# Inverting 64x64 blocks through their 32x32 diagonal blocks, with the full Gram products between the levels

## The chip, the core and the metric

The kernel runs on one core of one Trainium2 chip. The metric is the device time of one execution in microseconds (us). The core's engines run their own queues side by side and meet at semaphores: TensorE (PE; weight loads are shown apart as PEld), VectorE (DVE), ScalarE (ACT), GpSimd (POOL) and SyncE (SP), which issues most DMAs.

## What is computed

Two stacks of two layers on 256 tokens of width 1024. The first block (attention, spatial gating, a mixture of 64 experts) isn't touched. Each layer of the second block is `x + 0.5 swiglu(x)`, a mixer, and again `x + 0.5 swiglu(x)`. The mixer runs two branches on the projections of the normed x: differential attention over 4 head pairs, and an RWKV-7 recurrence in both directions over 8 heads of 64 channels:

```python
def step(state, inp):
    r_t, w_t, k_t, v_t, kk_t, a_t = inp
    sa = jnp.einsum('bhvk,bhk->bhv', state, -kk_t)
    state = (state * w_t[:, :, None, :]
             + sa[..., None] * (kk_t * a_t)[:, :, None, :]
             + v_t[..., None] * k_t[:, :, None, :])
    y_t = jnp.einsum('bhvk,bhk->bhv', state, r_t)
    return state, y_t
```

The result y gets a group norm, `ln_x`, the bonus `(r . k . r_k) v` and a gate; then `merged = sigmoid(gate_a) (o_a @ w_branch[0]) + sigmoid(gate_b) (o_b @ w_branch[1])`, and x + merged @ w_out. All is float32.

## The kernel before

The recurrence is cut into 4 chunks of CH = 64 tokens. Within a chunk, the effect of the sa terms on one another is a unit triangular 64x64 matrix for each head, chunk and direction, 64 of them a layer, whose inverse is wanted. They lie as two blocks in the 128 partitions and 8 columns of blocks (`u`), in four groups i = 2d + q: direction d, head half q. float32 matmuls stand in the trace as two pairs of weight load and matmul each.

The stages of one layer's mixer, all in `second_block`. Each engine has its own function (`tensor`, `scalar`, `vector`, `gpsimd`, `sync`), in which the order is written by hand, and `plan` deals the 8 PSUM banks out in the same order (`banks.take`); `claim` makes TensorE wait until a bank is freed, `read` makes another engine wait until it is filled, `evacuated` waits for the free.

- *Attention beside gates.* `score`, `turn_comb`, `values` of the 8 score tiles and 4 heads, with the gate projections in halves (`half_gates(i)`, L2122: 8 matmuls of 128x256) between them. VectorE makes softmax terms (`biased`, `combine`) and the scaled operands A, B, K, R (`keys`, `scaled`). TensorE waits for `kk_scaled` (L3040) before the products `kkb` (L2325), then come `score(2)`, the transposes of V and `half_gates(0)`. After `values(3)` come the token transposes (L2365) and the bonus sums (L2403).
- *Gram products* (`gram`, L2383 and L2379): UR and KR, 64x128 each, and L, 64x64, for each of the 64 blocks, masked out of PSUM by VectorE (`masked`: L3148, L3151) into UM, KM and X. GpSimd builds the start of the inverse and of its transpose from them (L2070 to L2072). The transposes of the attention output (`obT`, L2089) stand between the third and the fourth group and wait for VectorE's norm of it (`ob_ready`, L3169).
- *Levels*: five doublings on whole 64x64 blocks. In each, VectorE masks the level's part of U into Z (L3158), TensorE makes W = Z' X (`own_blocks`, L2393), ScalarE copies it to W1, TensorE makes dX and dXT, and VectorE adds them (L3188, L3192). One call of `own_blocks` is 16 matmuls of 64x64, 32 pairs, over two of the four 64x64 tiles of the array.
- *Q1, Atok, SA0, XAT* (L2443, L2450, L2393, L2467), all copied by ScalarE.
- *Scan* over 4 chunks (L2530 to L2549, L2480), with half_gates 10 to 13 one behind each chunk; then half_gates 14 and 15, the gate product (L2569), VectorE's group norm chain (L3243 to L3266), the transposes of the result (L2089), and `branch` (L2583), whose 8 output tiles each take 4 matmuls with either branch weight.

## Time and profile before

| | |
|---|---|
| median of 3 runs | 3445.56 us (3436.99 to 3446.21) |
| the profiled execution | 3436.36 us, its span 3434.5 us |
| TensorE busy | 3151.6 us, 92% |
| VectorE, ScalarE, GpSimd busy | 1494.9, 802.7, 636.4 us |
| mean granted TensorE clock | 0.946 of 2.4 GHz |
| the first layer's stage from the first Gram product to the scan | 2248 to 2344 us |
| the same in the second layer | 3022.5 to 3118 us |

Durations in a timeline row are those of a merged group: the number behind x is how many instructions it holds, and in brackets stands how long the engine was idle before it and who released it. The granted clock is given as a share of 2.4 GHz; it has two levels, 1.0 and 0.5.

### The profile page before, as it was taken

What the parts mean: (1) busy time and instruction counts of PE and PEld (TensorE: products, weight loads), DVE (VectorE), ACT (ScalarE), POOL (GpSimd) and SP (SyncE); (2) the same over time, 40 slices, a digit from 0 to 9 for tenths busy, and PEclk for the clock granted to TensorE, in tenths of its full rate; (3) what the DMA queues carried; (4) which work ended last, traced back from release to release, by engine and by line L of the source; (5) the groups of instructions that cost most, each with busy time, mean ns of one, the idle gap of its engine ahead of it and who ended that gap; (6) DMA issues with size and microseconds to landing.
All of it is one profiled execution on the core that took longest, in us unless ns stands there. A gap on an engine that the chain in (4) does not pass through costs nothing. (4 is left out here: it accounts for less than half of the span.)

```text
span 3434.5 us, 51714 instructions
## 1 busy us (share of the span) xinstructions
PE 3151.6 (92%) x22119; PEld 2147.9 (63%) x22119; DVE 1494.9 (44%) x2451; ACT 802.7 (23%) x1128; POOL 636.4 (19%) x580
## 2 busy tenths in 40 slices
PE   7988999999788889999994999988999999988999
PEld 3765334433256553334442998787798898787798
DVE  2334333323353243233325556673454655773454
ACT  1211111111013011111111335422233434522232
POOL 3511233333155022333332000020000000020000
PEclk9978999999888889999997999899999999999999
DMA  8635999999966369999997543202454553202452
GB/s 296 239 114 216 407 376 395 385 383 377 371 224 232 142 254 402 380 379 385 380 383 287 198 170 117 74 27 93 154 184 159 192 174 139 74 27 88 156 188 86
DMA packets 305358, 799.19 MB, mean 233 GB/s; under 512 B 57038, under 2 KB 155876, under 8 KB 251244
## 3 DMA queue, kind: packets, MB, share of 16 engines
q1 hardware_dynamic: 245804, 727.16, 56.3%
q0 software_dynamic: 58784, 66.64, 5.9%
q8 instruction: 177, 2.90, 0.3%
q10 hardware_dynamic: 544, 2.10, 0.2%
q14 instruction: 49, 0.40, 0.0%
HBM read 988.60 MB, written 53.48 MB: 303 GB/s over the span
## 5 line engine op out<-in xcount | busy, mean ns | idle before, releaser
L808 PE MATMUL f_bank<-f_ringA,f_arena 128*64 128x512 f32 x3072 | 688.0, 601 | 14.8 <-DMA f_ringA<-in_w_up,f_chosen 10.4
L808 PEld LDWEIGHTS f_bank<-f_ringA,f_arena 128*64 128x64 f32 x3072 | 218.3, 138 | 404.4 <-issue 403.3
L2133 PE MATMUL s_bank<-s_hT_parts,s_highA_parts 128*128 128x256 f32 x1344 | 380.7, 283 | 0.0
L2133 PE MATMUL s_bank<-s_hT_high_parts,s_ringA_parts 128*128 128x256 f32 x1344 | 380.6, 283 | 0.0
L2133 PE MATMUL s_bank<-s_hT_high_parts,s_highA_parts 128*128 128x256 f32 x1344 | 380.6, 283 | 0.0
L829 PE MATMUL f_bank<-f_ringB,f_arena 128*64 128x512 f32 x1536 | 346.3, 592 | 2.1 <-DVE f_arena L1595 2.1
L1580 DVE TENSOR_TENSOR f_arena<-f_arena,f_bank 128x256 f32<-128x256 f32 x96 | 58.7, 612 | 594.0 <-ACT f_arena L1190 594.0
L1111 ACT ACTIVATE f_arena<-f_bank 128x512 f32<-128x512 f32 (+1 forms) x266 | 144.8, 583 | 605.6 <-PE f_bank L789 323.3
L2133 PEld LDWEIGHTS s_bank<-s_hT_high_parts,s_highA_parts 128*128 128x128 f32 x1344 | 258.2, 192 | 1.4
L2133 PEld LDWEIGHTS s_bank<-s_hT_parts,s_highA_parts 128*128 128x128 f32 x1344 | 258.1, 192 | 1.4
L2133 PEld LDWEIGHTS s_bank<-s_hT_high_parts,s_ringA_parts 128*128 128x128 f32 x1344 | 258.1, 192 | 0.0
L829 PEld LDWEIGHTS f_bank<-f_ringB,f_arena 128*64 128x64 f32 x1536 | 112.3, 137 | 218.6 <-issue 216.0
L2930 DVE TENSOR_TENSOR s_ringA_parts<-s_ringA,s_highA_parts 128x4096 fp32r<-128x4096 f32 x44 | 194.7, 4424 | 61.2 <-ACT s_highA_parts L2624 60.9
L1589 DVE TENSOR_TENSOR f_arena<-f_bank,f_gate_b 128x512 f32<-128x512 f32 x192 | 132.9, 692 | 173.8 <-PE f_bank L829 156.9
L1190 ACT ACTIVATE f_arena<-f_bank 128x256 f32<-128x256 f32 x96 | 36.9, 385 | 657.8 <-PE f_bank L808 657.8
L2942 DVE TENSOR_TENSOR s_ringB_parts<-s_arena,s_highB_parts 128x2048 fp32r<-128x2048 f32 x44 | 100.8, 2292 | 193.4 <-ACT s_highB_parts L2634 193.1
L2624 ACT ACTIVATE s_highA_parts<-s_ringA 128x4096 fp32r<-128x4096 f32 x44 | 159.1, 3615 | 91.5 <-DMA s_ringA<-in_ffn_in 77.1
L2634 ACT ACTIVATE s_highB_parts<-s_arena 128x2048 fp32r<-128x2048 f32 x44 | 84.2, 1914 | 389.9 <-PE s_bank L2203 382.8
L2612 ACT ACTIVATE s_arena<-s_bank 128x512 f32<-128x512 f32 (+2 forms) x178 | 99.3, 577 | 259.3 <-PE s_bank L2393 87.2
L769 PE MATMUL f_bank<-f_hT,f_ringA 128*128 128x256 f32 x640 | 157.3, 409 | 2.7 <-ACT f_arena L1111 2.7
L682 POOL DMA_INDIRECT y_rows<-f_arena,f_rows_of x96 | 100.9, 1051 | 290.4 <-PE f_bank L789 231.8
L2070 POOL TENSOR_TENSOR s_arena<-s_arena,s_masks 128x512 f32<-128x512 f32 x8 | 11.1, 1383 | 747.2 <-DVEq L3153 747.2
(416 smaller groups left out, 5145.7 us busy)
## 6 DMA issues: line engine op xcount, KB each, us to landing
f_ringA<-in_w_gate SPq DMA_DIRECT2D x128, 1024.0 KB
f_ringA<-in_w_up SPq DMA_DIRECT2D x128, 1024.0 KB
f_ringB<-in_w_down SPq DMA_DIRECT2D x128, 1024.0 KB
s_ringA<-in_ffn_in SPq DMA_DIRECT2D x88, 1024.0 KB, 7.7
f_ringA<-in_w_ada SPq DMA_DIRECT2D x46, 1024.0 KB, 13.4
s_arena<-in_ffn_out SPq DMA_DIRECT2D x44, 1024.0 KB, 6.5
s_ringA<-in_w_in SPq DMA_DIRECT2D x40, 1024.0 KB, 6.2
f_ringA<-in_w_in SPq DMA_DIRECT2D x28, 1024.0 KB, 14.0
```

The lines of the kernel that those rows point to most:

```text
L682: pool.indirect_dma_start(out=a["y_rows"], out_offset=bass.IndirectOffsetOnAxis(ap=row_out[:, b:b + 1], axis=0), in_=y_tok[:, b % 3, :, :] ...
L769: last = mm(ps[:, t * S:(t + 1) * S], w[:, k, t * P:(t + 1) * P], hT[:, k, :], start=(k == 0), stop=(k == DT - 1))
L808: last = mm(ps[j * CAP:(j + 1) * CAP, :].rearrange("p (h c) -> p h c", h=2), picked[:, b % 2, k, j * CAP:(j + 1) * CAP], gu[j][:, :, k, :] ...
L829: last = mm(ps[j * CAP:(j + 1) * CAP, :], hidT[:, k, j * CAP:(j + 1) * CAP], wd[j][:, k, n * 512:(n + 1) * 512], start=(k == 0), stop=(k = ...
L1111: banks.free(f(dst, view(banks.read(act, key)), func), key)
L1589: banks.free(tt(y_tok[:, (b - 1) % 3, n, :], ps[:, :], gate_b[:, n * 512:(n + 1) * 512], ALU.mult), key)
L2133: last = mm(ps[:, t * S:(t + 1) * S], parts_of(wx[:, k, cs_]), parts_of(hx[:, k, :]), start=(k == 0 and x == 0), stop=(k == DT - 1 and x = ...
L2612: banks.free(f(dst, view_(banks.read(act, key)), func, **kw), key)
L2624: f(parts_of(highA[:, s % 2, :]), slotA(n), ACT.Copy).then_inc(highA_ready, 1)
L2634: f(parts_of(highB[:, s % 2, :]), ringB[:, s % B_SLOTS, :], ACT.Copy).then_inc(highB_ready, 1)
L2930: tt(parts_of(w), w, parts_of.value(highA[:, s % 2, :]), ALU.subtract).then_inc(lowA_ready, 1)
L2942: tt(parts_of(w), w, parts_of.value(highB[:, s % 2, :]), ALU.subtract).then_inc(lowB_ready, 1)
```

## The change

On VectorE, ScalarE and TensorE the inversion now works on the two 32x32 diagonal blocks of each 64x64 block (SUB = 32), through four levels, and a last step makes the off-diagonal 32x32 block. In detail:

- Small Gram products (`small_gram`) give L and U of the diagonal 32x32 blocks alone, side by side in one bank per (q, hh). ScalarE copies U to Uc, VectorE masks the start X and its transpose XX out of the same bank and adds the unit. GpSimd's twelve operations a layer are gone, and the L products of 64x64.
- A level handles both directions together: for each q one W of 64 matmuls (`quarters`: 32x32 blocks over the four diagonal tiles), one copy by ScalarE, and for each group one bank D with both updates, 64 matmuls, added by VectorE in one operation. VectorE's level mask covers both directions.
- The 16 full Gram products UR and KR (one bank each, `gram(name, d, q, hh)`) stand four to a level between W and D; VectorE masks them there. They were ahead of the levels.
- The last step: `last_level_left` (W5), `inverse_whole` (a selecting matmul of 256 columns puts the diagonal blocks into PSUM), `last_level_right` (adds the off-diagonal part), copied by ScalarE and VectorE to XT. The obT transposes follow.
- VectorE takes half of the copies of Q1, Atok, SA0 and XAT.
- Order on TensorE: kkb behind half_gates(0); bonus and the first token transposes ahead of half_gates(8); the small Gram products ahead of turn_comb(3), which moves combine(3) on VectorE behind the first start masks; half_gates 12 and 13 from the scan to its end.
- `branch` goes by weight: four tiles with the first, the same four with the second, then the other four; each weight is waited for where it is first used.
- VectorE: two of the operations behind the scan (bonus times V, plus the bias) are done ahead of it into yadd, and the mean's scaling is folded into the subtraction. ScalarE takes the square root for the group norm ahead of the last two gate copies, and runs the early gates' sigmoids in levels 2 and 3.

```diff
-        LEVELS = 5
+        LEVELS = 4
         scan_order = [list(range(NCH)), list(range(NCH))[::-1]]
         GATES_EARLY = 5
+        fillers = [(name, d, q, hh) for name in ("UR", "KR") for d in range(2) for q in range(2) for hh in range(2)]
...
                 pool.wait_ge(tables_landed, 4 * 16)
-                step = Chain(pool, pool_steps)
-                add = nc.gpsimd.tensor_tensor
-                unit = spread(masks[:, 12, :], 1, 8)
-                for d in range(2):
-                    for q in range(2):
-                        pool.wait_ge(u_ready, 2 * d + q + 1)
-                        step(add(XT[d][:, q], UM[d][:, q, :, 0, :], spread(masks[:, 6, :], 1, 8), ALU.mult))
-                        step(add(X[d][:, q], X[d][:, q], unit, ALU.add))
-                        add(XT[d][:, q], XT[d][:, q], unit, ALU.add).then_inc(start_ready, 1)
                 leave(pool, l)
...
-                half_gates(6)
-                turn_comb(2)
-                half_gates(7)
-                values(2)
-                half_gates(8)
-                turn_comb(3)
-                half_gates(9)
-                values(3)
...
+                def small_gram(q):
+
+                    ps = [banks.claim(pe, ("LU", q, hh)) for hh in range(2)]
+                    for d in range(2):
+                        for x in range(2):
+                            for a in range(2):
+                                for c in range(NCH):
+                                    for r in range(2):
+                                        s = slice(c * CH + r * SUB, c * CH + (r + 1) * SUB)
+                                        o = c % 2 * CH + r * SUB
+                                        n = 8 * d + 4 * x + 2 * a + c // 2
+                                        for hh in range(2):
+                                            h = slice(hh * HD, hh * HD + HD)
+                                            sides = AR[d][h, 2 * q + a, 0, s], Bt[d][h, 2 * q + a, s]
+                                            last = mm(ps[hh][o:o + SUB, n * SUB:(n + 1) * SUB], sides[x], sides[1 - x],
+                                                      start=True, stop=True)
+                                            if n == 15 and r == 1 and c == NCH - 1:
+                                                banks.fill(last, ("LU", q, hh))
+
+                def quarters(ps, at, left, right):
+
+                    for u in range(8):
+                        for o in range(0, P, SUB):
+                            last = mm(ps[o:o + SUB, (at + u) * SUB:(at + u + 1) * SUB], left[o:o + SUB, u],
+                                      right[o:o + SUB, u], start=True, stop=True)
+                    return last
 
...
+                tokens_first(0)
+                half_gates(8)
+                pe.wait_ge(ABKR_ready, 2)
+                for q in range(2):
+                    small_gram(q)
+                turn_comb(3)
+                half_gates(9)
+                values(3)
                 tokens_first(1)
-                gram(1, 0)
+
+                filler = iter(fillers)
+                for lv in range(LEVELS):
+                    for q in range(2):
+                        pe.wait_ge(z_ready, 2 * lv + q + 1)
+                        if lv:
+                            for i in (q, 2 + q):
+                                banks.evacuated(pe, ("D", i, lv - 1))
+                        else:
+                            pe.wait_ge(start_ready, 2 * q + 2)
+                        ps = banks.claim(pe, ("W", q, lv))
+                        for d in range(2):
+                            last = quarters(ps, 8 * d, Z[:, q, d], XX[d][:, q, 0])
+                        banks.fill(last, ("W", q, lv))
+                        gram(*next(filler))
+                    for q in range(2):
+                        banks.evacuated(pe, ("W", q, lv))
+                        for d in range(2):
+                            i = 2 * d + q
+                            ps = banks.claim(pe, ("D", i, lv))
+                            quarters(ps, 0, XX[d][:, q, 1], W1[:, q, d])
+                            banks.fill(quarters(ps, 8, W1[:, q, d], XX[d][:, q, 1]), ("D", i, lv))
+                        gram(*next(filler))
+
...
+                                src, to = o + d * SUB, o + (1 - d) * SUB
+                                other = slice((1 - d) * SUB, (2 - d) * SUB)
+                                last = mm(ps[to:to + SUB, u * SUB:(u + 1) * SUB], UM[d][src:src + SUB, q, u, 0, other],
+                                          XX[d][src:src + SUB, q, 0, u], start=True, stop=True)
+                    banks.fill(last, ("W5", q))
...
+                        ps = banks.claim(pe, ("XF", q, r))
+                        for d in range(2):
+                            for o in (0, CH):
+                                src = slice(o + r * SUB, o + (r + 1) * SUB)
+                                mm(ps[o:o + CH, d * S:(d + 1) * S], ident[src, o:o + CH],
+                                   XX[d][src, q, 1].rearrange("p u t -> p (u t)"),
+                                   start=True, stop=False, skip_group_check=True)
...
+                                r = 1 - d
+                                ps = banks.t[banks.uses[("XF", q, r)][0]]
+                                src, to, at = o + r * SUB, o + d * SUB, d * S + u * SUB
+                                last = mm(ps[to:to + SUB, at:at + SUB], W5[src:src + SUB, q, u],
+                                          XX[d][src:src + SUB, q, 1, u], start=False, stop=True, skip_group_check=True)
+                                if u == 7 and o == CH:
+                                    banks.fill(last, ("XF", q, r))
+
+                last_level_left(0)
+                inverse_whole(0)
+                last_level_left(1)
...
-                    half_gates(2 * GATES_EARLY + n)
+                    if n < 2:
+                        half_gates(2 * GATES_EARLY + n)
                 pe.wait_ge(sa_ready, 2 * (NCH - 1))
                 for d in range(2):
                     last = from_steps(d, NCH - 1)
                     banks.fill(last, ("YA", scan_order[d][NCH - 1] // 2))
-                half_gates(14)
-                half_gates(15)
+                for i in range(12, 16):
+                    half_gates(i)
                 for m in range(MT):
                     ps = banks.claim(pe, ("gate", m))
...
-                for t in range(DT):
-                    ps = banks.claim(pe, ("branch", t))
+                for first in (0, 4):
                     for half, (n, src) in enumerate(((a_wa, oaT), (a_wb, obT))):
+                        landed(n)
                         w = slotA(n).rearrange("p (k c) -> p k c", k=4)
-                        for k in range(4):
-                            last = mm(ps[:, half * S:(half + 1) * S], w[:, k, t * P:(t + 1) * P], src[:, k, :],
-                                      start=(k == 0), stop=(k == 3))
-                    banks.fill(last, ("branch", t))
+                        for t in range(first, first + 4):
+                            ps = banks.t[banks.uses[("branch", t)][0]] if half else banks.claim(pe, ("branch", t))
+                            for k in range(4):
+                                last = mm(ps[:, half * S:(half + 1) * S], w[:, k, t * P:(t + 1) * P], src[:, k, :],
+                                          start=(k == 0), stop=(k == 3))
+                            if half:
+                                banks.fill(last, ("branch", t))
...
+                def start_whole(i):
+
+                    xx = XX[i // 2][:, i % 2].rearrange("p x u t -> p (x u) t")
+                    for hh in range(2):
+                        banks.evacuated(dve, ("LU", i % 2, hh))
+                    tt(xx, xx, spread(small_masks[:, 4, :], 1, 16), ALU.add).then_inc(start_ready, 1)
+                        combine(3)
+                    for i in (q, 2 + q):
+                        start_whole(i)
                 for m in range(MT):
                     ps = banks.read(dve, ("o", m))
                     banks.free(v.tensor_copy(ob[:, m, :], ps[:, :]), ("o", m))
                     banks.evacuated(dve, ("o", m))
...
+                def level_mask(q, lv):
+
+                    of_level = small_masks[:, 5 + 2 * lv:7 + 2 * lv, :].unsqueeze(2).broadcast_to([P, 2, 8, SUB])
+                    tt(Z[:, q], Uc[:, q], of_level, ALU.mult).then_inc(z_ready, 1)
+
+                banks.evacuated(dve, "bonus")
+                filler = iter(fillers)
+                for q in range(2):
+                    level_mask(q, 0)
+                for lv in range(LEVELS):
+                    for _ in range(2):
+                        masked(*next(filler))
+                    for q in range(2):
+                        if lv < LEVELS - 1:
+                            banks.read(dve, ("W", q, lv))
...
-                step(ts(small[:, 120:136], small[:, 120:136], 1.0 / HD, None, ALU.mult))
-                step(tt(t1, yh, spread(small[:, 120:136], 2, HD), ALU.subtract))
+                step(stt(t1, spread(small[:, 120:136], 2, HD), -1.0 / HD, yh, ALU.mult, ALU.add))
...
                 step(tt(ym, ym, spread(lnx[:, 0, :], 1, MT), ALU.mult))
-                step(tt(ym, ym, spread(lnx[:, 1, :], 1, MT), ALU.add))
-                step(tt(t2, Vtok.rearrange("p m (h d) -> p (m h) d", d=HD), spread(small[:, 240:256], 2, HD),
-                        ALU.mult))
-                step(tt(ytmp, ytmp, ytmp2, ALU.add))
+                step(tt(ytmp, ytmp, yadd, ALU.add))
```

## Rows read from the trace of the kernel before

**Rows 1.** The page's busy times of the whole span.
```profile
PE 3151.6 (92%) x22119; PEld 2147.9 (63%) x22119; DVE 1494.9 (44%) x2451; ACT 802.7 (23%) x1128; POOL 636.4 (19%) x580
```

**Rows 2.** Busy time by stage, second block's mixer; columns in the first line.
```profile
core 0: us, PE busy (x) PEld busy (x) DVE busy (x) ACT busy (x) POOL busy (x), PEclk, DMA share, GB/s
...
2248.00:2272.00 24.00, 17.48 (x411) 16.08 (x411) 18.28 (x27) 5.04 (x9) 12.73 (x9) 0.79 0.01 3
...
2285.00:2297.00 12.00, 12.00 (x419) 12.00 (x416) 9.00 (x13) 2.91 (x5) 0.00 (x0) 1.00 0.02 4
...
2272.50:2330.20 57.70, 54.51 (x1792) 54.13 (x1794) 40.98 (x56) 15.94 (x26) 4.45 (x3) 0.97 0.02 4
...
2330.20:2343.90 13.70, 12.62 (x407) 11.48 (x402) 0.74 (x2) 9.56 (x24) 0.00 (x0) 1.00 0.02 5
...
2380.60:2400.80 20.20, 10.87 (x46) 8.36 (x45) 14.28 (x16) 4.38 (x7) 0.00 (x0) 0.84 0.60 218
...
3046.50:3104.30 57.80, 54.18 (x1804) 53.83 (x1797) 41.50 (x58) 15.93 (x26) 5.16 (x4) 0.97 0.02 4
```

**Rows 3.** Timeline of the Gram stage: start, duration, engine, line, operands, idle before.
```profile
2265.38 1.97 PE L2089 MATMUL s_bank<-ident,s_arena 128*128 128x128 f32 x8 [5.52 <-DVE s_arena L3169]
```

**Rows 4.** Timeline, weight loads: 128 columns, 64 at full and at half clock.
```profile
2244.45 3.09 PEld L2403 LDWEIGHTS s_bank<-s_rksel,s_arena 128*128 128x128 f32 x27
...
2257.39 1.76 PEld L2383 LDWEIGHTS s_bank<-s_arena 64*64 64x64 f32 x64 [0.24 <-issue]
...
2259.08 0.64 PEld L2379 LDWEIGHTS s_bank<-s_arena 64*64 64x64 f32 x32
...
2267.57 3.32 PEld L2383 LDWEIGHTS s_bank<-s_arena 64*64 64x64 f32 x64 [0.62 <-issue]
```

**Rows 5.** DMA queues, 2285 to 2330: the instruction queue's packets, MB, share.
```profile
q8 instruction: 11, 0.18, 1.7%
```

**Rows 6.** Timeline before the Gram stage, TensorE and VectorE.
```profile
2187.88 3.78 PE L2325 MATMUL s_bank<-s_arena,s_headselT 8*128 8x256 f32 x8 [4.15 <-DVE s_arena L3040]
...
2209.49 0.66 PE L2302 MATMUL s_bank<-ident,s_arena 128*128 128x128 f32 x4 [0.54 <-DVE s_arena L3082]
...
2233.68 1.05 PE L2312 MATMUL s_bank<-s_arena 128*128 128x128 f32 x8
...
2235.64 0.88 DVE L3082 SCALAR_TENSOR_TENSOR s_arena<-s_arena,s_small 128x256 f32<-128x256 f32 x2
```

**Rows 7.** Busy time by stage at the low clock (columns as in rows 2).
```profile
2247.70:2251.10 3.40, 3.40 (x57) 3.38 (x60) 0.53 (x1) 1.68 (x3) 0.00 (x0) 0.50 0.02 5
...
2268.00:2271.00 3.00, 3.00 (x64) 3.00 (x60) 1.08 (x3) 0.00 (x0) 2.40 (x2) 0.50 0.00 0
...
2394.50:2404.70 10.20, 5.89 (x17) 4.76 (x18) 3.26 (x4) 1.19 (x2) 0.00 (x0) 0.50 1.04 388
```

**Rows 8.** Timeline, changes of tile shape behind the levels.
```profile
2331.25 0.66 PE L2450 MATMUL s_bank<-ident,s_arena 128*128 128x128 f32 x4
...
2331.83 1.01 PEld L2443 LDWEIGHTS s_bank<-s_arena 64*64 64x64 f32 x32 [0.17 <-issue]
```

**Rows 9.** Groups by line, 1500 to 3434: VectorE on 128x512.
```profile
L3158 DVE TENSOR_TENSOR s_arena<-s_arena,s_masks 128x512 f32<-128x512 f32 x40 | 36.7, 936 | 7.3 <-PE s_bank L2393 6.7
...
L3192 DVE TENSOR_TENSOR s_arena<-s_bank,s_arena 128x512 f32<-128x512 f32 x40 | 27.7, 692 | 15.2 <-PE s_bank L2393 15.2
```

**Rows 10.** Timeline after the scan.
```profile
2380.59 7.17 PE L2122 MATMUL s_bank<-s_hT,s_ringA 128*128 128x256 f32 x32
...
2381.87 1.39 DVE L3243 TENSOR_TENSOR s_arena<-s_bank,s_arena 64x512 f32<-64x512 f32 x2 [7.49 <-ACT s_arena L2612]
...
2394.02 1.22 DVE L3261 TENSOR_TENSOR s_arena<-s_arena,s_small 128x1024 f32<-128x1024 f32 x1
...
2397.93 1.97 PE L2089 MATMUL s_bank<-ident,s_arena 128*128 128x128 f32 x8 [8.45 <-DVEq L3269]
...
2400.78 24.40 PE L2583 MATMUL s_bank<-s_arena,s_ringA 128*128 128x256 f32 x103 [0.89 <-ACT s_arena L2612]
```

More of the change, by code:

```diff
@@ L1667, in second_block @@
         masks = sb("masks", [P, 13, CH])
+        SUB = CH // 2
         dist = sb("dist", [P, MT, S])
@@ L2334, in tensor @@
                 half_gates(0)
+                pe.wait_ge(kk_scaled, 1)
+                for g in range(2):
+                    ps = banks.claim(pe, ("kkb", g))
+                    for t in range(2):
+                        last = mm(ps[:, t * S:(t + 1) * S], headselT[:, 2 * g + t, :], kk_norm, start=True, stop=True)
+                    banks.fill(last, ("kkb", g))
                 score(3)
@@ new lines, in scalar @@
+                take("bonus", bonus, lambda ps: ps[:, 0:16].rearrange("p (m h) -> p m h", m=MT))
+                tokens_first(0)
+                for q in range(2):
+                    for hh in range(2):
+                        ps = banks.read(act, ("LU", q, hh))[:, :].rearrange("p (d x n t) -> p d x n t", d=2, x=2, n=4)
+                        f(Uc[:, q, :, 4 * hh:4 * hh + 4, :], ps[:, :, 1], ACT.Copy).then_inc(u_ready, 1)
+                combined(3)
+                take_gates(4, ACT.Copy)
@@ new lines, in scalar @@
+                take(("Q1", 0), Q1[0], lambda ps: ps[:, :].rearrange("p (u c) -> p u c", u=8))
+                for q in range(2):
+                    ps = banks.read(act, ("XF", q, 0))
+                    for d in range(2):
+                        f(XT[d][:, q, :, 0:SUB], ps[:, d * S:(d + 1) * S].rearrange("p (u t) -> p u t", u=8), ACT.Copy
+                          ).then_inc(inv_ready[0], 1)
+                    act.wait_ge(inv_ready[0], 2 * q + 2)
+                    banks.free(act.nop(), ("XF", q, 0))
```

412 lines of the change are left out of this document (220 added, 192 removed).

## The prediction

> **What bounds the kernel now.** I read the busy shares first: TensorE is busy 92% of the span [rows 1], so the question is which work leaves its queue, and where it stands idle. The busy table by stage [rows 2] cuts the second block's mixer of the first layer (the second repeats it 774 us later; its level stage is the last row there). The level stage, 2272.5 to 2330.2, takes 57.7 us at 94% busy, with VectorE at 41 and ScalarE at 16: TensorE bounds it by instruction count, 1792 pairs of weight load and matmul, 29 ns each (12 us for some 415 of them). The Gram stage before it, 2248 to 2272, is bound by waits: TensorE is busy 17.5 of 24 us at a mean clock of 0.79, and its longest stop, 5.5 us, is for the vector chain that ends in L3169 [rows 3]. A third idle place, after the scan, is taken up in step 4.
>
> **The pace of a 32x32 pair** decides the change, and no row shows one. Its ends come from the loads' start spacing [rows 4]. Weight loads of 128 columns on the whole array come every 112 ns (3.09 us for 27). Loads of 64 columns come every 29 ns with two array tiles in use [rows 2], so 58 ns for each tile, and every 16 ns with four (0.64 us for 32, less the last one's own 0.13): 64 per tile. Per tile the time is a straight line in the columns: 58 at 64, 112 at 128, so 31 at 32. With the four diagonal tiles of a 32x32 block that is 7.8 ns per pair: the lower end. The upper end is 16, about the closest that pairs ever stand over a group of 32. Code loading lies between: eleven 16 KB blocks in 45 us took 1.7% of 16 engines, 1.1 us each [rows 5]; the 3584 instructions of the level stage are 254 a block at that rate. Loaded one behind the other, that is 8.7 ns per pair. I take 10, nearest to this row with a little room.
> The Trainium skill speaks against the change here: "TensorEngine Tiling (Array Packing)", section Instruction Overhead, says that each matmul carries about 60 cycles, so that 1 and 60 columns cost the same. That is 25 ns at 2.4 GHz; the 16 ns of the four-tile group does not agree with it as a limit on the queue.
>
> **The change part by part, one layer.** Times are those of the first layer.
> 1. *Before the levels.* Now the levels begin at 2272.5. VectorE is busy almost without a gap to 2236.5 (its third combine, L3082) and TensorE follows it: the first comb transpose starts on its release at 2209.49, and the third head's values start at 2233.68 [rows 6]. Moving score, V transposes and the first gate half ahead of the kk wait covers 4.15 us of idleness, but the same time is idle again before that comb transpose: nothing gained, -1 to +2 for a colder start. From the end of the values at 2234.6: bonus 4.0, first token transposes 1.9 plus 1.5 because the clock falls behind the bonus (it fell to 0.50 at 2247.7, right after it [rows 7]), half a gate 3.6, and 256 pairs of small Gram products at 10 ns, 2.5: 2248.1. These have two halves of rows and four of columns in use, 4 to 16 ns a pair: 1.0 to 4.1. VectorE's third combine now stands behind the first two start masks: copy on ScalarE 0.75, four masks of 0.41, combine 2.1: 2252.6. Behind that TensorE has transposes 0.6, half a gate 3.6, values 1.05: 2257.8; VectorE's two copies of o (1.4) and one level mask (0.7), with 0.3 of signalling, put the first level at 2260.2. That is 12.3 earlier, and neither GpSimd's start chain nor the obT transposes are before it.
> 2. *Levels.* Five levels become four. Each has 256 pairs in W and 512 in the two updates, 7.7 us at 10 ns, against 384 before: twice the instructions. Four full Gram products ride in each as fillers: 16 pairs of 128 columns over two tiles. Four tiles took 27 ns a pair at full clock (1.76 us for 64 [rows 4]), so two take 53: 0.85 us each, 3.4 in all. Each filler changes the tile shape twice. A change from 64x64 to 128x128 costs 0.16 us between loads [rows 8]; eight cost 1.4 with rounding up, 0 if these two shapes need none. A level is 12.5 us, four are 50.0 against 57.7. The Trainium skill ("TensorEngine Tiling (Array Packing)", Key Properties) states that changing the tiling mode drains the array; the 0.16 us agrees.
> Cover: VectorE has ten operations of 128x512 a level, 0.69 each as L3192 [rows 9], 7.2 us; L3158 took 0.94 in the mean only beside GpSimd, which is now idle. Group norm work adds 2.7 us behind level 0 and 2.9 in level 2. Total 34.5 of 50, so no stall until a pair falls below 7. ScalarE's two copies have a filler and the other W behind them. Range of the four levels: 43 (7.8 ns; 38 if the shape changes are free) to 68 (16).
> 3. *From the levels to the scan*, 13.7 us now. The last level, which joins the two 32-wide halves, is 256 pairs (2.6) and 32 selecting pairs of 256 columns over two tiles, 107 ns each (3.4). Moved here from the Gram stage are the obT transposes, 0.9. The rest is as now: four Q1 and four SA0 of 0.93 each, 3.7 and 3.7, XAT 4 times 0.5, transposes 1.7, eleven shape changes 1.8, final wait 1.3. Sum 21.1: 7.4 later. VectorE takes half of the copies, 3.0 us a pair of heads against 4.6 on TensorE. The two new yadd operations (1.22 each, as L3261 [rows 10]) stand before the first state, 0.9 us late, behind which TensorE has from_keys and half a gate: nothing.
> 4. *After the scan.* Two of the gate halves leave it: VectorE's answers have landed behind the remaining from_steps, so the scan ends 7.2 earlier (four halves then follow; two take 7.17 [rows 10]). They run beside the norm chain, where TensorE waits 8.45 now. From the last YA product, branch starts at 20.2 now [rows 2]. After: gates 14.4, gate product 1.9, VectorE's last gate multiply 0.9, transposes 1.0, copies 1.0: 19.3. The chain itself loses 2.7 us (three operations) and is no longer last. The branch's first 4 us run at half clock now, since the clock is 0.50 from 2394.5 to 2404.7 [rows 7]; without the idleness 2.0 are saved. Splitting branch by weight hides the second weight load: it is issued when the last gate ends, +14.4, and has until about +26.7. Sum: -10.1.
> **Sum.** -12.3 - 7.7 + 7.4 - 10.1 = -22.7 a layer, -45 in two. Against the profiled execution, 3436.4 us, that is 3391. This execution lies 9 below the median of the runs, 3445.6, so I put the median after at **3400**.
>
> **Rivals.**
> *A, the array's own line (7.8 ns or a little more).* 3328 pairs a layer hang on the pace, plus 256: 3.6 us for each ns. 2.2 ns less are 16 us in two layers: 3384. For: pairs in a group start together, waiting for the tile only. Against: no longer stretch shows it.
> *B, the sequencer or code loading holds about 14 to 16 ns.* 3.6 x 2 x 4 to 6 = +29 to +43: 3429 to 3443. Break-even is at 16.3 ns. For: it is the closest spacing seen. Against: that spacing is just what four 64-column tiles allow.
> *C, slower: the clock falls in the levels.* The clock fell behind the bonus though its loads kept the queue full (8 columns each), and in the gappy start of the levels; the 32-column pairs use a sixteenth of the array each. At half clock a pair is 16 ns and a filler 1.7 (64 pairs took 3.32 us for 1.76 [rows 4], the clock at 0.50 there [rows 7]): 20.5 us a level, +32 a layer: 3464. It eats the whole gain when about 70% of the level time is at the low level. Against: the 64x64 pairs, a quarter of the array each, hold 1.00 for 50 us, and the fillers stand between.
> *D, slower by far: the queue delivers no faster than now.* 29 ns is the only pace that the trace holds over hundreds of pairs; if it is the queue's and not the tiles', each 32x32 pair costs it: 19 x 3.6 x 2 = +137: 3537. For: the groups at 16 ns are only 32 pairs long and could be drawn from a filled queue. Against: they stand at it right behind long stretches at 29. With the 25 ns of the Trainium skill ("TensorEngine Tiling (Array Packing)", Instruction Overhead) the same mechanism would give 3508.
> *E, steps 1 to 3 don't do what they say:* waits that the sum doesn't have eat them and only step 4 stays, 10 us a layer: 3425, beside B.
>
> **How the numbers follow.** Forecast (9 to 12 ns) 0.42, 3386 to 3417; A 0.20; B with E 0.24; C in part or whole 0.10; D 0.04. Of C about a half is a partial fall that leaves the time within or below the old one. A with free shape changes and a good early stage reaches 3372; B ends at 3443. Range 3372 to 3443. A measurement here tells 0.3%, 10 us, from no change. Faster by more than that: forecast, A and most of B, 0.77; within: the end of B, part of C, 0.12; slower: C, D, 0.11.
>
> **What would show it.** The level stage: four levels, each with 768 pairs, length 50 us; the spacing of the 32x32 loads, 10 ns; granted clock 1.00 in it. The levels' start 12 us earlier relative to the comb transposes; TensorE idle some 4 us before the last comb transpose. The stage from the last level to the scan at 21 us. After the scan, no idle time over 1.5 us on TensorE until branch, and full clock in it. GpSimd with no tensor operation, VectorE's level masks at 0.69. The prediction is wrong if the pairs stand at over 13 ns, if VectorE or ScalarE ends the waits in the levels, or if the clock is 0.50 in them.

## The result, and the profile after

| | us | |
|---|---|---|
| before | 3441.56 | median of 4 runs, 3436.99 to 3446.21 |
| after | 3506.24 | median of 4 runs, 3498.87 to 3507.56 |
| ratio | 1.018 | 95% interval 1.016 to 1.021 |
| profiled execution after | 3507.32 | span 3505.5, mean clock 0.923 (before: 0.946) |

The change costs 65 us. The forecast was a gain of some 45, and the time is outside its range. The page of after, busy times and the instruction queue, to be read against [rows 1]:

```profile
PE 3193.1 (91%) x26023; PEld 2170.6 (62%) x26023; DVE 1456.2 (42%) x2425; ACT 789.6 (23%) x1104; POOL 599.0 (17%) x556
...
q8 instruction: 207, 3.39, 0.4%
```

TensorE has 3904 more pairs of load and matmul than before. In the table of the first layer's stages (columns as in [rows 2]) the rows are: the small Gram products, the four levels, the way to the scan, the scan, and the stretch from the last YA product to branch:

```profile
2247.40:2260.00 12.60, 5.87 (x513) 5.42 (x512) 4.57 (x13) 0.66 (x2) 0.00 (x0) 0.66 0.02 4
2270.00:2366.90 96.90, 76.26 (x3329) 67.29 (x3328) 30.34 (x44) 10.55 (x17) 0.00 (x0) 0.54 0.02 4
2366.90:2388.80 21.90, 20.40 (x697) 17.28 (x697) 7.92 (x18) 8.49 (x21) 0.00 (x0) 0.91 0.02 5
2388.80:2418.50 29.70, 28.53 (x673) 26.27 (x673) 10.85 (x24) 0.60 (x1) 0.00 (x0) 1.00 0.20 73
2418.50:2437.20 18.70, 16.84 (x77) 13.67 (x77) 11.75 (x13) 6.15 (x9) 0.00 (x0) 1.00 0.18 60
```

Against [rows 2]: the levels begin 2.5 us earlier (2270.0 for 2272.5), last 96.9 us in place of 57.7, the way to the scan takes 21.9 for 13.7, and from the scan's start on 10.4 us are won (scan 29.7 for 36.7, stretch to branch 18.7 for 20.2, branch itself 27.9 for 29.8). That is -2.5 + 39.2 + 8.2 - 10.4 = +34.5 us a layer, 69 in two; the two profiled executions differ by 71.0. So **the whole loss, and more, is in the level stage**, where VectorE is busy 30 and ScalarE 11 of 97 us.

What TensorE waits for there stands in the costliest groups (busy us, mean ns of one, then idle time before it and its releaser), both layers together:

```profile
L2391 PE MATMUL s_bank<-s_arena 32*32 32x32 f32 x6144 | 94.6, 233 | 36.2 <-issue 36.0
L2364 PE MATMUL s_bank<-s_arena 64*64 64x128 f32 x512 | 61.1, 403 | 5.0 <-issue 4.9
L2382 PE MATMUL s_bank<-s_arena 64*32 64x32 f32 x1024 | 11.8, 229 | 12.8 <-issue 12.8
```

"Issue" is a stop for nothing that the profile shows: no engine, no data. In the first layer's level stage these stops sum to 20.6 us. The timeline tells their rhythm. First the small Gram products (L2382), then the beginning of the levels (start, duration, line, count, idle before):

```profile
2247.43 1.74 PE L2382 MATMUL s_bank<-s_arena 64*32 64x32 f32 x182
2251.44 1.61 PE L2382 MATMUL s_bank<-s_arena 64*32 64x32 f32 x128 [2.27 <-issue]
2255.32 1.55 PE L2382 MATMUL s_bank<-s_arena 64*32 64x32 f32 x128 [2.26 <-issue]
2259.06 1.04 PE L2382 MATMUL s_bank<-s_arena 64*32 64x32 f32 x74 [2.20 <-issue]
...
2270.01 1.29 PE L2391 MATMUL s_bank<-s_arena 32*32 32x32 f32 x128
2271.22 0.66 PE L2364 MATMUL s_bank<-s_arena 64*64 64x128 f32 x8
...
2280.84 1.74 PE L2391 MATMUL s_bank<-s_arena 32*32 32x32 f32 x128 [0.53 <-issue]
2284.59 0.39 PE L2391 MATMUL s_bank<-s_arena 32*32 32x32 f32 x25 [2.00 <-issue]
...
2288.32 1.93 PE L2391 MATMUL s_bank<-s_arena 32*32 32x32 f32 x128 [0.69 <-issue]
2292.34 0.79 PE L2391 MATMUL s_bank<-s_arena 32*32 32x32 f32 x41 [2.09 <-issue]
```

Two things are to be seen. At the full clock 128 of the 32x32 pairs are through in 1.21 us (2270.01 to 2271.22), 9.5 ns each: the pace that was forecast at 10. And TensorE stops for 2 us again and again, each time 128 pairs, 256 instructions, after the last stop. 256 instructions are one 16 KB packet of the instruction queue; in the level stage (2270.0 to 2366.9) this queue has 26 of them (packets, MB, share):

```profile
q8 instruction: 26, 0.43, 1.9%
```

Put beside each other, the starts of TensorE's instructions counted in 256s, and the starts of the packets in that queue (both from the trace, us; the stop here runs from the start of one instruction to the start of the next, so it is some 0.2 longer than the idle time in brackets above):

```
after, levels
block taken up at   stop before it   own work of the block before   next packet starts   and takes
2251.44             2.47             1.08                           +1.14                1.29
2255.32             2.50             1.37                           +1.16                1.11
2259.06             2.43             1.31                           +1.07                1.38
2284.59             2.19             1.55                           +1.41                1.07
2292.34             2.33             1.69                           +1.18                0.94
2299.52             0.00             3.57                           +1.41                0.88
2307.09             2.05             1.69                           +1.12                1.36
```

A packet starts some 1.15 us after TensorE has taken up a block, moves in 0.9 to 1.4, and TensorE goes on 2.6 us after the packet's start. So the next block can be taken up some 3.75 us after this one (3.5 to 4.3 over the stage, its first block apart, which took 2.9). If this block has 3.6 us of work there is no stop (the sixth line, at the half clock); if it has 1.5, TensorE stands for the rest. The level stage has 4 x 1664 = 6656 instructions, 26 blocks: 26 x 3.75 = 97.5 us, and it took 96.9. At the half clock, though, many blocks of this stage have just 3.6 us of work of their own, so this sum alone doesn't tell blocks from the clock; the experiments have to.

The rule of the Trainium skill that bears on it ("Runtime: NRT & Kernel Launch", section Instruction fetch mechanics) says that a queue of the sequencer's own loads the next 16 KB block while the present one is executed; the table agrees. It also says that this is hidden, because instructions issue more slowly than the blocks come; that does not hold here: 256 instructions of these pairs are executed in 1.3 us and their successors come in 3.75.

### The profile page after: what moved, and what is told of

The parts are those of the page before. It is cut to its first block and busy times, and to the rows that moved or that the text cites. A ratio compares the mean times of both kernels' runs of the same rounds, so it can differ in the third digit from the quotient of the medians.

```text
span 3505.5 us, 59420 instructions
## 1 busy us (share of the span) xinstructions
PE 3193.1 (91%) x26023; PEld 2170.6 (62%) x26023; DVE 1456.2 (42%) x2425; ACT 789.6 (23%) x1104; POOL 599.0 (17%) x556
## 5 line engine op out<-in xcount | busy, mean ns | idle before, releaser
L2701 ACT ACTIVATE s_arena<-s_bank 128x512 f32<-128x512 f32 (+2 forms) x142 | 78.9, 575 | 324.2 <-PE s_bank L2391 139.1
L769 PEld LDWEIGHTS f_bank<-f_hT,f_ringA 128*128 128x128 f32 x640 | 131.4, 207 | 27.2 <-ACT f_arena L1111 4.0
```

The source lines that it names most:

```text
L769: last = mm(ps[:, t * S:(t + 1) * S], w[:, k, t * P:(t + 1) * P], hT[:, k, :], start=(k == 0), stop=(k == DT - 1))
L2701: banks.free(f(dst, view_(banks.read(act, key)), func, **kw), key)
```

## The experiments

Theories: **T1**, TensorE waits for blocks of instructions; **T2**, the clock, 0.54 in the levels, makes them long; **T3**, each 32x32 product has its price in the array. The kernel before alone took 3425 to 3448 us over all its runs, so a difference of some 10 us between two single runs says nothing; the stage lengths are surer.

**Same instructions, twice the array work (`wide`).**

```diff
                     for u in range(8):
+                        v = u // 2 * 2
                         for o in range(0, P, SUB):
-                            last = mm(ps[o:o + SUB, (at + u) * SUB:(at + u + 1) * SUB], left[o:o + SUB, u],
-                                      right[o:o + SUB, u], start=True, stop=True)
+                            last = mm(ps[o:o + SUB, (at + v) * SUB:(at + v + 2) * SUB], left[o:o + SUB, u],
+                                      right[o:o + SUB, v:v + 2].rearrange("p u t -> p (u t)"), start=True, stop=True)
```

> The kernel after, with each 32x32 product of the levels made 64 columns wide (it reads and writes two neighbouring products' columns), so the values of the levels are wrong, and the number of instructions is the same: 4 levels of 832 loads and 832 matmuls, with the array's work in them doubled. Theory T1 (TensorE waits for its instructions, which come in blocks of 256, one every 3.75 us, whatever it computes): the four levels stay at 4 x 1664 / 256 x 3.75 = 97 us a layer, the kernel within 10 us of 3506, even if the granted clock in the levels rises from 0.50. Theory T2 (the half clock makes the levels long: the 32x32 pair takes 14.6 ns there and 9.4 ns at the full clock, and the idle gaps keep the clock low): more columns keep the clock up or, at the half clock, take 53 ns for a pair of two streams' worth, so the levels move by over 10 us either way. Theory T3 (a price of each 32x32 product in the array): doubled columns lengthen the levels, by up to 3072 x 13 ns = 40 us a layer at the full clock, kernel over 3550.

Measured: 3495.45 us, beside 3434.11 for before on that chip. The level stage of this kernel:

```profile
2261.00:2356.70 95.70, 70.10 (x3331) 61.60 (x3331) 30.34 (x44) 10.51 (x17) 0.00 (x0) 0.97 0.02 5
```

95.7 us with the array doing double and the clock at 0.97, against 96.9 at 0.54: T3 falls. The kernel is 11 us below after, a little more than T1 allowed, but 9 of these are there before the levels begin (2261.0 for 2270.0), ahead of any changed product. T2 has a way out that its wording missed: twice the columns at twice the clock would also take as long as before. What closes it is the idle time. TensorE is busy 70.1 of the 95.7 us, and the 25.6 us between are "issue" stops at every 256th instruction, as in after. Both layers' small products in the costliest groups:

```profile
L2392 PE MATMUL s_bank<-s_arena 32*32 32x64 f32 x6144 | 109.1, 224 | 45.0 <-issue 45.0
```

From 2261.0 to 2312.7 the clock is 1.00 throughout, and 15.1 us of such stops lie in these 51.7 us, so T2 falls too.

**Half the instructions, the same columns (`half`).** As `wide`, with `for u in range(0, 8, 2)`.

> The kernel after, with every second 32x32 product of the levels left out and the others 64 columns wide, so the values are wrong; the levels stream the same number of columns with 448 loads and 448 matmuls in place of 832 each. T1 (instruction blocks): 4 x 896 / 256 x 3.75 = 52.5 us of levels a layer in place of 97, the kernel at about 3506 - 2 x 44.5 = 3417. T2 (half clock, set by the columns streamed): the levels stay near 97 us if the clock stays at 0.50, the kernel near 3506.

Measured: 3419.1 us, 2 over T1's number. The level stage:

```profile
2270.10:2321.60 51.50, 43.26 (x1792) 36.92 (x1790) 29.79 (x44) 10.59 (x17) 0.00 (x0) 1.00 0.02 5
```

51.5 us where 14 blocks were to take 52.5, and the same columns streamed. By length alone the three stages would also fit columns streamed, divided by the clock (131 thousand columns at 0.54, 229 at 0.97, 131 at 1.00: 96.9, 95.7 and 51.5 us); the idle time, 25.6 us in `wide` and 8.2 here, at nearly the full clock, is what such a rule has no place for. Together with it, these lengths say that the number of instructions sets the time.

**Large useless products between the levels (`ballast`).** In the function of the full Gram products:

```diff
+                    for _ in range(2):
+                        mm(ps[:, :], ident[:, :], AR[d][:, 2 * q, :, :].rearrange("p r s -> p (r s)"), start=True, stop=True)
                     for a in range(2):
```

> The kernel after, with two useless 128x128 by 512-column products ahead of each of the 16 Gram products between the levels (32 a layer, two passes each, written to the bank that the Gram product then overwrites): 64 x 0.213 us = 13.7 us more work of TensorE a layer at the full clock, twice that at the half clock, in only 128 instructions, half a block. T1 (instruction blocks come at their own pace while TensorE computes): the levels stay at 97 us, at most 2 us more for the half block, and the work lies in the waits; the kernel within 5 us of 3506. T2 and T3 (TensorE is busy with the array's work in the levels): 14 us more a layer, the kernel at 3534; under T2 less where the clock comes back.

Measured: 3554.99 us, 49 over after's own median, where I expected no more than 5. Both halves of the expectation were off. A pass of 512 columns takes 0.5 us at the full clock and 0.85 at half, not 0.213, so the added work was some 45 us a layer:

```profile
L2361 PE MATMUL s_bank<-s_arena,ident 128*128 128x512 f32 x128 | 89.8, 839 | 0.9 <-issue 0.9
L2393 PE MATMUL s_bank<-s_arena 32*32 32x32 f32 x6144 | 70.0, 201 | 46.4 <-issue 46.4
```

Of these 45 us, 24 lengthened the level stage:

```profile
2272.70:2393.80 121.10, 96.71 (x3394) 61.84 (x3392) 30.32 (x44) 10.60 (x17) 0.00 (x0) 0.82 0.02 4
```

The rest did not go into the waits: TensorE is idle 24.4 us of this stage, where it was 20.6 in after. It was given back by the clock, 0.82 for 0.54, at which the stage's own products took some 25 us less. So the stops are all still there, 46 us in two layers. The timeline shows why:

```profile
2299.56 0.66 PE L2393 MATMUL s_bank<-s_arena 32*32 32x32 f32 x53 [2.48 <-issue]
2300.15 3.48 PE L2361 MATMUL s_bank<-s_arena,ident 128*128 128x512 f32 x4
...
2324.06 1.31 PE L2393 MATMUL s_bank<-s_arena 32*32 32x32 f32 x128 [1.12 <-issue]
2327.81 0.33 PE L2393 MATMUL s_bank<-s_arena 32*32 32x32 f32 x8 [2.43 <-issue]
2328.07 3.53 PE L2361 MATMUL s_bank<-s_arena,ident 128*128 128x512 f32 x4
...
2335.38 0.44 PE L2393 MATMUL s_bank<-s_arena 32*32 32x32 f32 x29 [1.80 <-issue]
```

The block taken up at 2327.8 has 5.6 us of own work and is followed by a stop all the same. The packets show why, if one counts how many of a block's instructions stand ahead of its first large product:

```
ballast, levels of both layers (us)
block taken up at   instructions ahead of the large product   next packet   next block
2369.08             10                                         +4.63         +7.04
2327.80             16                                         +4.99         +7.57
2279.40             24                                         +4.79         +7.37
3130.48             39                                         +5.30         +7.98
2379.59             51                                         +1.26         +7.21
2335.38             58                                         +1.05         +3.97
2290.24             65                                         +1.29         +5.55
2299.56            106                                         +1.07         +5.63
2295.79             none in this block                         +0.87         +3.77
```

The next block is asked for when TensorE's queue is some 40 to 50 instructions into the present one (late at 39, in time at 51). A large product ahead of that point holds the request back by its whole time and hides nothing; behind that point it hides up to 2 us. And nothing is loaded further ahead than one block: the block at 2346.68 took 5.6 us without a stop behind it, and yet the short one after it, at 2352.30, had to wait 2.1 us for its successor. So T1 was refined: each block costs the longer of about 3.75 us and its own work, one by one, and what a block has too much does nothing for the next.

**The same kind of work in small portions (`even`).** In the function of the 32x32 products:

```diff
+                    for _ in range(2):
+                        mm(ps[:, at * SUB:(at + 8) * SUB], ident[:, :], AR[0][:, 0, 0, :], start=True, stop=True)
                     for u in range(8):
```

> The kernel after, with useless work of TensorE again, now in small portions: two 128x128 by 256-column products ahead of every 32 of the 32x32 products, written to the columns that these then overwrite. By the run with 512 columns a pass of 512 took about 0.5 us at the full clock and 0.85 at half, so a pass of 256 about 0.25 to 0.43; 48 portions of 4 passes a layer are 48 to 82 us more work a layer, with 384 more instructions, 1.5 blocks. Theory T1 as the 512-column run leaves it (each block of 256 instructions is asked for when TensorE takes up the one before, is there 3.75 us later, and nothing is loaded further ahead, so a block costs the longer of 3.75 us and its own work): a block's work is 1.2 to 1.5 us and 2.0 to 2.3 portions, 3.3 to 3.8 us at the full clock, so nearly all of the added work lies in the waits: the levels 97 + 5.6 (1.5 blocks) = 100 to 112 us, the kernel 3515 to 3536. If blocks were loaded any number ahead, the levels are also near 103 us, and then the 16 large portions of the other run should have cost nothing, which they did not. If TensorE's own work fills the levels: 97 + 48 to 82 us, the kernel over 3600.

Measured: 3521.2 us. The level stage, and the groups of the useless and of the small products:

```profile
2273.10:2377.10 104.00, 101.80 (x3577) 77.91 (x3577) 31.03 (x45) 9.74 (x15) 0.00 (x0) 1.00 0.02 4
...
L2390 PE MATMUL s_bank<-s_arena,ident 128*128 128x256 f32 x384 | 108.3, 405 | 0.1
L2393 PE MATMUL s_bank<-s_arena 32*32 32x32 f32 x6144 | 74.4, 194 | 1.9 <-issue 1.5
```

54 us of useless work a layer lengthen the stage by 7 (1.5 blocks more would be 5.6), and nearly all stops in it are gone: TensorE is idle 2.2 us for 20.6. Some 18 of the 54 us thus lie in the former stops, and some 28 were offset by the clock, 1.00 for 0.54, at which the stage's own products take less. The expectation had put nearly all into the stops, so its number came out (3515 to 3536) in part for another reason, and by its time alone this run doesn't tell blocks from the clock; that rests on `wide`. It tells one more thing: the stage is now 98% busy at clock 1.00, so without the useless work the levels' own work is 104 - 54, some 50 us. That is the number of the prediction's step 2; it was TensorE's own work at the full clock, and that was not what bound.

**Do the old levels wait for instructions too?** Their pace, 29 ns a pair [rows 2], is also 3.7 us for 256 instructions. First half of the columns (`narrow`): `own_blocks` got a width, 32 in levels 1 to 4.

> The kernel before, with the 64x64 products of levels 1 to 4 streaming 32 columns in place of 64, so the values are wrong; the number of instructions is the same (896 products a layer, 3584 instructions). T1 (instruction blocks bind the old levels too): the level stage stays at 57.7 us, the kernel at 3441 plus or minus 5. If the array's time for a 64x64 product was the bound of the old levels, the 704 narrowed ones, two passes each, save up to 1408 x 13 ns = 18 us a layer, the kernel at about 3405.

Measured: 3438.34 us, T1's number, but the trace speaks against T1's reason:

```profile
2281.72 50.49 PE L2393 MATMUL s_bank<-s_arena 64*64 64x64 f32 x1696 [1.69 <-issue]
```

1696 pairs in one piece with no stop in it, 29.8 ns each, though most of them stream half the columns: neither streamed columns nor visible waits. Its weight loads kept their 64 columns; no run varies these alone. Then useless work ahead of each 16 products of the old kernel (`before_even`):

```diff
                 def own_blocks(ps, left, right):
+                    mm(ps[:, 0:S], ident[:, :], AR[0][:, 0, 0, :], start=True, stop=True)
```

> The kernel before, with one useless 128x128 by 256-column product (two passes, 0.265 us each at the full clock by the run even) ahead of each of the 60 calls that make 16 of the 64x64 products: 32 us more work a layer, 64 in all, with 240 more instructions a layer. If the array holds the old levels at 29 ns a product and instructions are only just in time (128 products take 3.7 us, the block's own 3.75), the work adds in full: the kernel at 3500. If the old levels too wait for their instructions, in a form that shows no pauses, the work lies in these waits: the kernel below 3450.

Measured: 3524.59 us beside 3424.82: the work adds in full, 100 us where its array time alone was put at 64. The timeline (the useless passes are L2391):

```profile
2360.29 1.15 PE L2394 MATMUL s_bank<-s_arena 64*64 64x64 f32 x32
2361.37 0.70 PE L2391 MATMUL s_bank<-s_arena,ident 128*128 128x256 f32 x2
2362.00 1.15 PE L2394 MATMUL s_bank<-s_arena 64*64 64x64 f32 x32
2363.08 0.70 PE L2391 MATMUL s_bank<-s_arena,ident 128*128 128x256 f32 x2
```

A call has 32 pairs, 0.94 us at 29.2 ns, and comes every 1.71 here: 0.77 more, 92 us for 120 calls, no part of it hidden. The instruction packets now come 5.3 to 7.4 us apart, so no block is waited for here, and 32 products still take 1.15 us. So it is the products themselves that hold the old levels at 29 ns, and their instructions come only just in time: 3.7 us of work for a block that takes 3.75. (In the second layer of `obt_late`, below, the old levels show two stops labelled "issue", 0.18 and 0.23 us, 126 pairs apart.) What in the products the 29 ns are, if not the columns streamed, stays open; the 64-column weight load is the candidate that no run tested.

**The edits behind the scan alone (`scan_end`).** Its diff is that of the change, limited to the gates' order and banks, branch by weight, and the bonus term and the shift made during the scan.

> The kernel before with the change's edits behind the scan alone: the halves of the gates 12 to 15 behind the scan, the gates' last group in another bank, ScalarE's roots ahead of the last two gate groups, VectorE's bonus term and shift made during the scan, one VectorE step in place of two, the branch matrices taken by weight. The levels stay as they were. The prediction's step 4 had 10.1 us a layer for these, 20 us in all: the kernel at 3421. If the gain of step 4 hung on the rest of the change, or the edits only move a wait: within 5 us of 3441.

Measured: 3413.38 us against 3434.59, ratio 0.994, interval 0.992 to 0.995: 21 us faster, 20 expected. Its end of the scan:

```profile
2376.20 14.08 PE L2123 MATMUL s_bank<-s_hT,s_ringA 128*128 128x256 f32 x64
2390.12 1.88 PE L2571 MATMUL s_bank<-s_g,s_arena 128*128 128x512 f32 x4
2392.82 1.09 PE L2090 MATMUL s_bank<-ident,s_arena 128*128 128x128 f32 x8 [0.83 <-DVEq L3273]
```

The four gate halves (first row) lie beside VectorE's norm chain, and the 8.45 us idle of [rows 10] are 0.83.

**A start for the old levels.** `obt_late` is `scan_end` with the obT transposes moved behind the levels, and VectorE's norm of them behind its last Gram masks, to take away the 5.5 us of [rows 3].

```diff
                 gram(1, 0)
-                pe.wait_ge(ob_ready, 1)
-                to_features(("obT",), ob, 2)
                 gram(1, 1)
...
+                pe.wait_ge(ob_ready, 1)
+                to_features(("obT",), ob, 2)
                 for m in range(MT):
```

> scan_end, and the 16 transposes of the second half's output moved from between the Gram products to behind the levels, with VectorE's five norm steps ahead of them moved behind its last Gram mask. TensorE waited 5.5 us there a layer and the transposes took some 2 us: if the Gram products bound the start of the levels, 7 us a layer less than scan_end, 3407; if VectorE's masks and GpSimd's starts bind it anyway, 0 to 3 us a layer, 3415 to 3421.

Measured: 3409.91 us, ratio 0.994, interval 0.992 to 0.995: not to be told from `scan_end`. The Gram products end early, and TensorE then stands before the fourth product, until GpSimd's last start value is there (its last row ends at 2269.4):

```profile
2267.08 2.33 POOL L2073 TENSOR_TENSOR s_arena<-s_arena,s_masks 128x512 f32<-128x512 f32 x1
...
2269.51 15.70 PE L2394 MATMUL s_bank<-s_arena 64*64 64x64 f32 x458 [4.10 <-issue]
```

Here "issue" does hide an engine: the row above names it. `start_split` is `obt_late` with the fourth start value given to VectorE.

```diff
                 level_mask(2, 0)
+                own = spread(masks[:, 12, :], 1, 8)
+                tt(XT[1][:, 1], UM[1][:, 1, :, 0, :], spread(masks[:, 6, :], 1, 8), ALU.mult)
+                step(tt(X[1][:, 1], X[1][:, 1], own, ALU.add))
+                tt(XT[1][:, 1], XT[1][:, 1], own, ALU.add).then_inc(start3_ready, 1)
                 level_mask(3, 0)
```

> The kernel obt_late with the start values of the fourth product made by VectorE (three steps of some 0.6 us between its last Gram masks and its last level mask) in place of GpSimd, which had them ready at 2269.4 in obt_late while TensorE had begun the first level at 2260.1 and stood 4.1 us ahead of the fourth product. If GpSimd's starts are what held the first level: the fourth product starts at about 2266, 3.3 us a layer earlier, and the kernel is at 3403 where obt_late has 3410. If VectorE becomes late instead (its masks for level 1 follow the norm steps): within 2 us of 3410.

Measured: 3405.68 us against 3437.22, ratio 0.990, interval 0.988 to 0.992. The fourth product's wait:

```profile
2267.07 2.15 PE L2394 MATMUL s_bank<-s_arena 64*64 64x64 f32 x64
2271.22 1.51 PE L2394 MATMUL s_bank<-s_arena 64*64 64x64 f32 x32 [1.99 <-DVE s_arena L3162]
2273.75 52.37 PE L2394 MATMUL s_bank<-s_arena 64*64 64x64 f32 x1696 [1.02 <-DVE s_arena L3162]
```

It starts 6.7 us after the first level's begin, where it was 9.4; what it waits for now is VectorE's mask (L3162). This is **the fastest version, 1% faster than before and 2.8% faster than after**, with the old levels and the new end. Against `scan_end` and `obt_late` the intervals just part (to 0.9916 here, from 0.9924 and 0.9922 there), between runs on two chips.

## Why the prediction was wrong

**The step that failed is the pace, in its code loading.** It had "1.1 us each" and "loaded one behind the other", 8.7 ns a pair. The 1.1 us is right as the time of a packet (0.9 to 1.4). That packets follow one another was nowhere in the rows; [rows 5] shows eleven in 45 us, one every 4.1, and I read their duration where their spacing was the safe number. A packet starts only when a block is taken up, and 1.15 + 2.6 us pass until its instructions run: 3.75 us a block, 14.6 ns an instruction, 29.3 a pair. So the forecast's 10 ns had to be compared with 29, not with 8.7.

**Rival D was the case, at a chance of 0.04.** It gave 29 ns and 3537 us. Its sentence for it ("the groups at 16 ns are only 32 pairs long and could be drawn from a filled queue") is what happens. It was too high by 31 us. It priced the wait pair by pair on top of the fillers, where the fillers' work lies inside the waits: 50 + 19 x 3.07 = 108 us for the levels, and they took 96.9, which is 23 of the 31 in two layers. Its stated reason against ("they stand at it right behind long stretches at 29") was no evidence: the old levels stand at 29 by the array, with their blocks in time, as `before_even` shows. Two limits, 3.7 and 3.75 us for 256 instructions, lay on top of each other in the trace of before, and I took them for one.

**Step 1, the earlier start:** -12.3 forecast, -2.5 measured. The three pieces before the small Gram products came as worked out but for 1.8 us (they began at 2247.4, not 2245.6). The products themselves are 512 pairs, not 256 (a miscount of the two passes), and took four blocks, 12.6 us for 2.5. Behind them 10.0 us to the levels for 12.1. The idle time before the first head's comb transpose is there, as step 1 had it (6.32 us for 4.15 and 0.54 before); the prediction's list of signs put it before the last comb transpose, which has none.

```profile
2206.92 1.11 PE L2298 MATMUL s_bank<-ident,s_arena 128*128 128x128 f32 x4 [6.32 <-DVE s_arena L3191]
```

**Step 2, the levels:** 50.0 forecast, 96.9 measured; as TensorE's own work at the full clock some 50 is right (`even`). VectorE and ScalarE ended no wait in them, as said.

**Rival C, the clock:** it did fall, to 0.50 over 85 us:

```profile
2285.50:2370.90 85.40, 70.16 (x2922) 61.03 (x2918) 27.98 (x41) 8.93 (x14) 0.00 (x0) 0.50 0.02 5
```

but it cost next to nothing: a block's 3.6 us of work at half clock still fits in 3.75, where the rival had 32 us a layer for it. `wide`, with double the columns, had the clock at 0.97 and took 1.2 us less. The stops alone don't explain the fall, since `wide` has more of them (25.6 us for 20.6); the stops together with the 32-column products were there when it fell.

**Step 3, to the scan:** 21.1 forecast, 21.9 measured. **Step 4, behind the scan:** -10.1 forecast, -10.4 measured, and 21 us for both layers with nothing else changed (`scan_end`). TensorE's two stops there are 0.83 and 1.05 us, and branch begins 18.7 after the last YA product (19.3 forecast).

Steps 3 and 4 held within 1 us. Of the 57 us a layer between forecast and result, 46.9 are in step 2 and 9.8 in step 1, whose small Gram products met the same wait; one assumption, the pace, is behind nearly all of it. The bound that the text itself had, 29 ns "the only pace that the trace holds over hundreds of pairs", should have been an end of the range; the range ended at 16 ns for a reason taken from groups of 32.

## What to carry to other kernels

Count the instructions of a stage of TensorE, divide by 256, and multiply by 3.75 us: on these traces no long stage of small products was shorter than some 0.98 of that, whatever its products cost, so splitting products into smaller ones pays only as long as a block's own work stays above that. Where such a stage can't be avoided, spread long products through it, a few in every 256 instructions (`even`); in one place they fill one block's wait alone, and within the first 40 or so instructions of a block not even that (`ballast`). Stops labelled "issue" that come at every 256th instruction are the sign, and the packets of the instruction queue, one for each 256 instructions, confirm it. A single run with more work per instruction proves little by its length, since the clock may rise with it; read its idle time too.

## What the runs showed of the hardware that was not expected

- Instructions: one block of 256 ahead at most, asked for 40 to 50 instructions into the present one, there 3.75 us (3.5 to 4.3 in after's level stage, its first block apart) after that one was taken up.
- 32x32 products on four diagonal tiles: 9.5 ns a pair. The Trainium skill ("TensorE: Matmul & The Clock Gate", section Back-to-back issue gap) puts matmuls of up to 64 columns at about 25 ns each; the 1.21 us for 128 of them does not agree.
- 64x64 products on two diagonal tiles: 29 to 30 ns a pair with 64 columns streamed or with 32, the weight load at 64 in both.
- A pass of 128x128 by 256 columns took 0.265 us in a group of four, one of 512 columns 0.5 at the full clock and 0.85 at half.
- The releaser "issue" stood for two things: a block of instructions that was not there, and in `obt_late` a wait for GpSimd's value, which the record did not name.
